# Router on unscaled rows, positions in bf16 and filler products: the routing section of a hybrid decoder on one core

## The chip, the cores and the metric

One Trainium2 chip, one of its cores. The core's engines are TensorE (PE, with its weight loads PEld), VectorE (DVE), ScalarE (ACT), GpSimd (POOL) and SyncE (SP), which here issues every DMA. The metric is the device time of one execution in microseconds (us), the median of several runs; lower is better. Everything is f32 except where bf16 is named.

## The reference, cut to what matters

Two identical layers work on 256 tokens of 1024 channels. Each layer adds three sub-layers to the residual stream `h`: token mixing, cross-attention into 256 memory tokens, and a mixture of 32 experts in 4 groups. The change sits between the second and the third.

```python
def hier_moe(xn, w_rg, b_rg, w_re, b_re, w_gu, w_dn):
    ...
    lg = jnp.dot(xf, w_rg).astype(jnp.float32) + b_rg.astype(jnp.float32)
    p_grp = jax.nn.softmax(lg, axis=-1)
    grp = jnp.argmax(lg, axis=-1)
    ...
    le = jnp.take_along_axis(le, grp[:, None, None], axis=1)[:, 0]
    top_p, top_e = lax.top_k(jax.nn.softmax(le, axis=-1), EXPERT_TOP_K)
    gate = p_grp_sel * top_p / jnp.sum(top_p, axis=-1, keepdims=True)
    ...
    gu = lax.ragged_dot(xs, w_gu, sizes)
    g_, u_ = jnp.split(gu, 2, axis=-1)
    ys = lax.ragged_dot(jax.nn.silu(g_) * u_, w_dn, sizes)
...
        h = h + cross_attention(rmsnorm(h, norm_cross[l]), rmsnorm(mem, norm_mem[l]),
                                cross_wq[l], cross_wkv[l], cross_wo[l])
        h = h + hier_moe(rmsnorm(h, norm_ffn[l]), router_group_w[l], router_group_b[l],
                         router_expert_w[l], router_expert_b[l], expert_w_gate_up[l], expert_w_down[l])
```

`rmsnorm(x, g)` is each row of x times 1/sqrt(mean of its squares), times the gain g of each channel. Every token goes to two experts of one group, and every expert's weights (6 MB) are read from HBM once a layer.

## The kernel before, in words

The kernel is one program written out by hand for each engine; the order on an engine is the order of its code, and semaphores tie the engines together. A name such as `h0_ffn` or `chosen` is such a semaphore event. The eight PSUM banks are shared by a table, `USES`: for each bank it lists its uses in order, and a use can be filled only after the one before it in the same bank has been drained.

The 256 tokens are two tiles of 128 (`tt` is 0 or 1). Behind cross-attention, PE multiplies the attention result by the output weights (`cross_out`, banks co0 to co3), and DVE adds that to `h` (`add_out`). Then, for each tile: ACT squares the rows (`squares`), DVE makes the inverse root (12 small instructions, `inverse_root`), ACT (tile 0) or DVE (tile 1) scales the rows into `xhat`, PE transposes `xhat` (`turn`, uses zT0 to zT3), DVE and ACT multiply the halves of the result by the gain into `xnT` (`turned`), and PE multiplies `xnT` by the 36 router columns (bank use `rt`).

DVE adds the bias and picks group and experts in some 20 small dependent instructions; their outcome is the table `chosen` (one where a token uses an expert). PE sums `chosen` with a triangle and with ones (use `pos`), which gives every token its place in its expert. From that DVE builds the one-hot matrix `pm` of the first pair of experts (`onehot(0)`), and PE gathers the rows of that pair by multiplying `xhat` with `pm` (`gather(0, 0)`, `gather(0, 1)`). DVE meanwhile orders the experts of each pair by size, counts the passes (`npass_ready`), and writes the tables of positions and gates of all pairs; then it multiplies the gathered rows by the gain (`gathered(0)`).

After that a loop runs over the 16 pairs of experts: gate and up products, SiLU on ACT, down products, and a product that scatters the result back to the tokens. SP loads the weights of the next pairs, each load behind the last read of the slot that it overwrites. The loads of pair 0 and most of those of pair 1 are issued before routing; the first one behind them waits for `small_read`, which PE raises when the first half of pair 0's gate and up products is done. Each layer has this sequence once. In layer 0 POOL also makes the gained memory of layer 1 (`gained(xnT, 1)`, L1212), released by `npass_ready`.

## Time and profile before

| | |
|---|---|
| median of 3 runs | 1445.12 us (1444.04 to 1446.16) |
| profiled execution, its own time | 1444.26 us |
| its span, first to last instruction | 1442.1 us |
| busy in the span: PE, DVE, ACT, POOL | 1243.6, 496.2, 243.4, 81.2 us |
| mean of PE's granted clock, as a share of full speed | 0.955 |
| mean HBM read and written | 315 GB/s |

The profiled execution's own time is 2.16 us above its span (what lies before the first and behind the last instruction), and 0.86 us below the median of the runs. Times inside the span are counted from its start. Layer 0's experts begin at about 275 us, layer 1's at about 978 us. A clock of 1.00 is 2.4 GHz and one of 0.50 is 1.2 GHz; there are only these two levels, so a share between them is a stretch with both.

### The profile page before, as it was taken

The numbers are of one execution on the slowest core, as the hardware profiler recorded it, in microseconds if no ns is written. First come the engines' busy times: TensorE is split into PE (matmuls) and PEld (weight loads), VectorE is DVE, ScalarE is ACT, GpSimd is POOL, SyncE is SP. The second block draws the span as 40 slices with busy tenths as digits, with TensorE's granted clock in tenths as the row PEclk, the third lists the DMA queues.
The fourth block names the chain that finished last, engine by engine and source line by source line (L and its number), as shares of the span: only waits on it lengthen the run. The fifth ranks groups of instructions, "written<-read, shape, count | busy, mean of one in ns | idle before, by whom it ended". The sixth has DMA issues, their size and how long they took to land.

```text
span 1442.1 us, 26136 instructions
## 1 busy us (share of the span) xinstructions
PE 1243.6 (86%) x10690; PEld 739.3 (51%) x10690; DVE 496.2 (34%) x1113; ACT 243.4 (17%) x564; POOL 81.2 (6%) x105
## 2 busy tenths in 40 slices
PE   4989898699899898878889889969988998798885
PEld 3877756444444343434468776655444443344332
DVE  4254634433223222322242654353223232222323
ACT  2003213011111111111120221221111111111111
POOL 1121300000000000000021222000000000000000
PEclk9999999699999999999999999979999999999997
DMA  8231229299999999999944113567999999999993
GB/s 337 93 147 59 102 82 428 81 426 428 427 386 428 428 427 427 428 428 429 423 174 166 60 59 117 246 279 298 425 428 385 428 429 427 429 427 427 429 428 147
DMA packets 33103, 455.11 MB, mean 316 GB/s; under 512 B 3744, under 2 KB 4000, under 8 KB 5152
## 3 DMA queue, kind: packets, MB, share of 16 engines
q1 hardware_dynamic: 33056, 454.46, 75.4%
q8 instruction: 32, 0.52, 0.1%
q14 instruction: 15, 0.12, 0.0%
HBM read 453.40 MB, written 1.05 MB: 315 GB/s over the span
## 4 chain that ended last, share of the span: by engine, by line
PE 48%; DMA 39%; DVE 6%; ACT 2%; issue 2%; SPq 1%; DVEq 0%; ACTq 0%
PE bank L459 47%; DMA share<-in_w_gu 30%; DMA share<-in_w_dn 9%; SPq L370 1%; ACT xnT L1044 1%; DVE small L1469 1%; PE bank L518 1%; DMA lb_in<-in_lb_logits 1%; DVE share L1449 1%; PE bank L677 1%; DVE rest L1760 0%; DVE h L1401 0%; ACT ring L1098 0%; DVE rest L1690 0%; ACT xhat L1025 0%
## 5 line engine op out<-in xcount | busy, mean ns | idle before, releaser
L459 PE MATMUL bank<-share,rest 128*32 128x512 f32 (+1 forms) x2560 | 309.6, 531 | 16.5 <-DMA share<-in_w_dn 16.4
L459 PE MATMUL bank<-ring,rest 128*32 128x256 f32 (+1 forms) x1792 | 184.5, 492 | 35.9 <-DMA share<-in_w_gu 30.4
L459 PE MATMUL bank<-dense,rest 128*32 128x256 f32 (+2 forms) x1824 | 190.3, 480 | 24.6 <-DMA share<-in_w_gu 21.9
L459 PE MATMUL bank<-xnT,dense 128*128 128x256 f32 (+2 forms) x960 | 162.4, 344 | 13.4 <-ACT xnT L1044 6.3
L459 PEld LDWEIGHTS bank<-share,rest 128*32 128x32 f32 x2560 | 102.7, 113 | 111.7 <-issue 94.8
L459 PEld LDWEIGHTS bank<-xnT,dense 128*128 128x128 f32 (+1 forms) x960 | 140.5, 179 | 32.2 <-issue 13.3
L459 PE MATMUL bank<-rest 96*128 96x512 f32 (+1 forms) x288 | 122.0, 579 | 34.3 <-DVE rest L1760 34.3
L459 PEld LDWEIGHTS bank<-ring,rest 128*32 128x32 f32 x1792 | 66.7, 113 | 156.0 <-issue 98.8
L1751 DVE TENSOR_TENSOR rest<-rest,bank 64x512 f32<-64x512 f32 x64 | 35.7, 558 | 322.3 <-ACT rest L1175 296.0
L459 PEld LDWEIGHTS bank<-dense,rest 128*32 128x32 f32 (+1 forms) x1824 | 69.6, 112 | 146.5 <-issue 97.8
L459 PE MATMUL bank<-rest,xhat 128*128 128x96 f32 x1088 | 142.2, 286 | 2.7 <-DVE rest L1679 2.7
L459 PEld LDWEIGHTS bank<-rest,xhat 128*128 128x128 f32 x1088 | 131.5, 198 | 18.2 <-issue 16.1
L1768 DVE TENSOR_TENSOR h<-h,bank 128x512 f32<-128x512 f32 x128 | 88.0, 688 | 57.4 <-PE bank L459 57.4
L459 PEld LDWEIGHTS bank<-rest 96*128 96x128 f32 (+1 forms) x288 | 48.8, 189 | 95.9 <-issue 95.7
L1175 ACT ACTIVATE rest<-bank 64x512 f32<-64x512 f32 x32 | 18.8, 588 | 444.7 <-PE bank L459 444.7
L1734 DVE TENSOR_TENSOR rest<-bank,par 128x384 f32<-128x384 f32 x68 | 37.8, 558 | 104.6 <-PE bank L459 103.3
L459 PE MATMUL bank<-dense,ring 128*32 128x128 f32 (+1 forms) x384 | 63.0, 380 | 0.0
L1757 DVE COPY rest<-bank 64x512 f32<-64x512 f32 x32 | 22.2, 693 | 109.0 <-PE bank L459 109.0
L459 PE MATMUL bank<-share 64*128 64x128 f32 (+2 forms) x448 | 41.3, 311 | 13.7 <-DVE ring L1544 7.2
L459 PE MATMUL bank<-dense,xnT 128*128 128x256 f32 (+2 forms) x256 | 46.4, 341 | 5.6 <-DVE share L1449 3.5
L1181 ACT ACTIVATE rest<-bank 64x512 f32<-64x512 f32 x32 | 18.9, 590 | 184.2 <-PE bank L459 184.2
L459 PEld LDWEIGHTS bank<-dense,xnT 128*128 128x128 f32 x256 | 41.1, 195 | 10.2 <-issue 3.9
(229 smaller groups left out, 954.9 us busy)
## 6 DMA issues: line engine op xcount, KB each, us to landing
share<-in_w_dn SPq DMA_DIRECT2D x64, 2048.0 KB, 19.8
ring<-in_w_gu SPq DMA_DIRECT2D x48, 2048.0 KB, 23.7
dense<-in_w_gu SPq DMA_DIRECT2D x48, 2048.0 KB, 26.6
share<-in_w_gu SPq DMA_DIRECT2D x32, 2048.0 KB, 22.9
dense<-in_w_units SPq DMA_DIRECT2D x18, 2048.0 KB, 9.0
dense<-in_w_units SPq DMA_DIRECT2D x4, 1024.0 KB, 5.1
dense<-in_w_units SPq DMA_DIRECT2D x2, 1184.0 KB, 5.8
ring<-in_w_units SPq DMA_DIRECT2D x2, 1024.0 KB, 5.8
```

Of the source, the lines that this page charges most:

```text
L370: e = sp.value_load(order_i[0:1, bass.ds(pair * 2 + s % 2, 1)], min_val=0, max_val=E - 1)
L459: return pe.matmul(out_ap, lhsT=lhsT, rhs=rhs, start=start, stop=stop, skip_group_check=True)
L518: ins = pe.transpose(bk[:, d * P:(d + 1) * P], xhat[:, tt, k * P:(k + 1) * P], ident)
L677: ins = pe.transpose(bk[:, c * P:(c + 1) * P], probs(n)[:, at:at + P], ident)
L1044: ins = act.activation(xnT[:, 4 + d, tt * P:(tt + 1) * P], bk[:, d * P:(d + 1) * P], ACT.Identity, scale=pcol(l, gain + 4 + d, 1))
L1175: act.activation(sgate[UP, 0:512], banks[2][0:HD, 0:512], ACT.Silu).then_inc(edrained[2], 1)
L1181: act.activation(ys[0:HD, 0:512], banks[4][0:HD, 0:512], ACT.Copy).then_inc(edrained[4], 1)
L1449: bank_drained(V.copy_predicated(a01[:, :, half, :], bc(lvmask[:, m, :].unsqueeze(1), 4, P), bk[:, 0:512].rearrange("p (n t) -> p n t", n= ...
L1734: V.tensor_tensor(xg[:, 4 * b:4 * b + 4, :], banks[b][:, 0:4 * ROWS].rearrange("p (d s) -> p d s", d=4), g, MUL).then_inc(edrained[b], 1)
L1751: V.tensor_tensor(hid[UP, c0:c1], sgate[UP, c0:c1], banks[b][UP, 0:c1 - c0], MUL).then_inc(edrained[b], 1)
L1757: V.tensor_copy(ys[0:HD, 512:1024], banks[4][UP, 0:512]).then_inc(edrained[4], 1)
L1768: V.tensor_tensor(hh, hh, banks[b][:, 0:512], ADD).then_inc(edrained[b], 1)
```

## The change

It has four parts, all between cross-attention and the loop over the pairs, and a small one in the preparation.

1. The router's transposes read `h` itself. The two tiles' logits are multiplied by the rows' scale afterwards, in DVE's instruction that also adds the bias. So the transposes no longer wait for the root; the scaled rows `xhat` are still made, both tiles now by ACT and behind `turned`, for the gather. `zT0` and `zT1` move to banks 4 and 5, and the first tile's transposes stand ahead of `cross_out(1)`.
2. `chosen` becomes a bf16 table, `chosen_b`, and the triangle and the ones of the positions product come from bf16 constants (`cbf`, 544 columns for 288).
3. PE multiplies constants into bank 2, whose content nobody reads: 18 products of 128x512 in bf16 ahead of the positions product, 4 behind it, and 4 behind the first gather.
4. DVE writes the tables of all pairs behind `gathered(0)`, no longer ahead of it, and POOL's product of layer 1's gained memory waits until DVE has made the gated one-hots of pair 1.

```diff
@@ USES @@
-        "wo0", "wo2", "yT0", "cq0", "yT2", "co0", "co2", "zT0", "zT2"],
+        "wo0", "wo2", "yT0", "cq0", "yT2", "co0", "co2", "zT2"],
...
-    4: ["hq", "hidT", "rk", "cmp_t"] + [f"t{n}_0" for n in range(NG)],
+    4: ["hq", "hidT", "rk", "cmp_t"] + [f"t{n}_0" for n in range(NG)] + ["zT0"],
...
@@ preparation @@
-        cbf = sb("cbf", [P, 288], BF16)
+        cbf = sb("cbf", [P, 544], BF16)
+        chosen_b = sb("chosen_b", [P, 2, 32], BF16)
...
-            sp.dma_start(rest[:, 0:1312], masks).then_inc(s_setup, 16)
+            sp.dma_start(rest[:, 0:1568], masks).then_inc(s_setup, 16)
@@ TensorE @@
-                def turn(prefix, stage, tt):
+                def turn(prefix, stage, tt, rows=xhat):
 
-                    wait(f"xhat{tt}_{stage}")
+                    wait(f"xhat{tt}_{stage}" if rows is xhat else f"h{tt}_{stage}")
...
+                turn("z", "ffn", 0, h)
                 cross_out(1)
 
                 bk = bank_free(pe, l, "rt")
-                for tt in range(2):
-                    turn("z", "ffn", tt)
+
+                def route(tt):
                     settled(f"zT{2 * tt}", f"zT{2 * tt + 1}")
                     for k in range(8):
                         ins = mm(bk[:, tt * 36:(tt + 1) * 36], xnT[:, k, tt * P:(tt + 1) * P],
                                  pcol(l, RW + k * 36, 36), k == 0, k == 7)
-                bank_done(ins, "rt")
+                    return ins
+
+                route(0)
+                turn("z", "ffn", 1, h)
+                bank_done(route(1), "rt")
+
+                def keep_clock(n):
+
+                    for i in range(n):
+                        mm(banks[2][:, 0:512], ident_b, cbf[:, 0:512], True, True)
+
+                wait_drained(pe, l, USES[2][-1])
+                keep_clock(18)
 
                 wait("chosen")
                 bk = bank_free(pe, l, "pos")
-                mm(bk[:, 0:E], tri, chosen[:, 0, :], True, True)
...
+                mm(bk[:, 0:E], tri_b, chosen_b[:, 0, :], True, True)
...
                 bank_done(ins, "pos")
+                keep_clock(4)
...
+                wait("xhat0_ffn")
+                wait("xhat1_ffn")
                 gather(0, 0)
                 gather(0, 1)
+                keep_clock(4)
                 wait("npass_ready")
@@ ScalarE @@
                 norm("ffn", 0)
+                turned("z", G_FFN, 0)
                 norm("ffn", 1)
-                turned("z", G_FFN, 0)
                 turned("z", G_FFN, 1)
+                for tt in range(2):
+                    wait(f"rstd{tt}_ffn")
+                    act.activation(xhat[:, tt, :], h[:, tt, :], ACT.Identity,
+                                   scale=rs[:, tt:tt + 1]).then_inc(ev(f"xhat{tt}_ffn"), 1)
@@ GpSimd @@
                 if l + 1 < DEPTH:
-                    wait("npass_ready")
+                    pool.wait_ge(pg_of[l], 2)
+                    alone(pool)
                     gained(xnT[:, :, :], l + 1).then_inc(ev("memG"), 1)
@@ VectorE @@
+                turned("z", G_FFN, 0)
                 norm("ffn", 0)
                 add_out("co", "ffn", 1)
-                turned("z", G_FFN, 0)
+                turned("z", G_FFN, 1)
                 norm("ffn", 1)
-                turned("z", G_FFN, 1)
...
-                bank_drained(V.tensor_tensor(rl, bk[:, 0:72].rearrange("p (t c) -> p t c", t=2),
-                                             bc(pcol(l, RBIAS, 36).unsqueeze(1), 2, 36), ADD), "rt")
+                for tt in range(2):
+                    ins = V.scalar_tensor_tensor(rl[:, tt, :], bk[:, tt * 36:(tt + 1) * 36], rs[:, tt:tt + 1],
+                                                 pcol(l, RBIAS, 36), MUL, ADD)
+                bank_drained(ins, "rt")
...
-                own("chosen", V.tensor_tensor(chosen, r_o1, r_o2, ADD))
+                V.tensor_tensor(chosen_b[:, :, :], r_o1, r_o2, ADD).then_inc(ev("chosen"), 1)
```

The first place is PE from the last values product of cross-attention to the router's products. Of before (`xhat` are the scaled rows, `par,xnT` the router's products, `dense,rest` the products of `cross_out(1)`):

```order
L459 MATMUL bank<-xnT,rest 64x128 x7
L459 MATMUL bank<-dense,rest 128x512 [waits bank0_drained,bank7_drained]
L459 MATMUL bank<-dense,rest 128x512
L459 MATMUL bank<-dense,rest 128x512 [waits bank1_drained]
L459 MATMUL bank<-dense,rest 128x512
L518 MATMUL bank<-cst,xhat 128x128 [waits bank0_drained,xhat0_ffn,bank6_drained]
L518 MATMUL bank<-cst,xhat 128x128 x3
L518 MATMUL bank<-cst,xhat 128x128 [waits bank1_drained]
L518 MATMUL bank<-cst,xhat 128x128 x3
L459 MATMUL bank<-par,xnT 128x36 [waits bank1_drained,bank0_drained]
```

Of the changed kernel, the same stretch:

```order
L462 MATMUL bank<-xnT,rest 64x128 x7
L521 MATMUL bank<-cst,h 128x128 [waits bank4_drained,h0_ffn]
L521 MATMUL bank<-cst,h 128x128 x3
L521 MATMUL bank<-cst,h 128x128 [waits bank5_drained]
L521 MATMUL bank<-cst,h 128x128 x3
L462 MATMUL bank<-dense,rest 128x512 [waits bank0_drained,bank7_drained]
L462 MATMUL bank<-dense,rest 128x512
L462 MATMUL bank<-dense,rest 128x512 [waits bank1_drained]
L462 MATMUL bank<-dense,rest 128x512
L462 MATMUL bank<-par,xnT 128x36 [waits bank4_drained,bank5_drained,bank6_drained]
```

The transposes of tile 0 have moved ahead of the four products of `cross_out(1)`, and the first router product follows those directly.

The second place is PE from the second tile's router products to the read of `npass`. Of before (`rest,cst` is the positions product, `rest,xhat` the gather):

```order
L459 MATMUL bank<-par,xnT 128x36 x7
L459 MATMUL bank<-rest,cst 128x32 [waits bank1_drained,chosen]
L459 MATMUL bank<-rest,cst 128x32 x4
L459 MATMUL bank<-rest,xhat 128x96 [waits bank5_drained,bank6_drained,bank4_drained,bank7_drained,bank3_drained,onehot_ready_0,bank2_drained,ebank0_drained_0,bank1_drained,bank0_drained]
L459 MATMUL bank<-rest,xhat 128x96 x7
L459 MATMUL bank<-rest,xhat 128x96 [waits ebank1_drained_0]
L459 MATMUL bank<-rest,xhat 128x96 x7
L914 TENSOR_LOAD npass_i [waits npass_ready]
```

Of the changed kernel (`cbf` are the bf16 constants, `bank<-cbf 128x512` the filler products):

```order
L462 MATMUL bank<-par,xnT 128x36 x7
L462 MATMUL bank<-cbf 128x512 [waits bank2_drained]
L462 MATMUL bank<-cbf 128x512 x17
L462 MATMUL bank<-chosen_b,cbf 128x32 [waits bank1_drained,chosen]
L462 MATMUL bank<-chosen_b,cbf 128x32 x4
L462 MATMUL bank<-cbf 128x512 x4
L462 MATMUL bank<-rest,xhat 128x96 [waits bank6_drained,bank7_drained,bank5_drained,xhat0_ffn,bank4_drained,xhat1_ffn,bank3_drained,onehot_ready_0,bank2_drained,ebank0_drained_0,bank1_drained,bank0_drained]
L462 MATMUL bank<-rest,xhat 128x96 x7
L462 MATMUL bank<-rest,xhat 128x96 [waits ebank1_drained_0]
L462 MATMUL bank<-rest,xhat 128x96 x7
L462 MATMUL bank<-cbf 128x512 x4
L933 TENSOR_LOAD npass_i [waits npass_ready]
```

The filler products stand in PE's queue ahead of the wait for `chosen`, ahead of the gather's wait and ahead of the read of `npass`, so each of these now also waits for them.

The third place is DVE ahead of `gathered(0)`, the two rows `rest<-bank,par` that wait for the halves of the gather. Of before (`posv` and `gates` are the tables of all pairs):

```order
L1691 TENSOR_REDUCE posv<-rest 128x16x2 [waits dve_step]
L1690 TENSOR_TENSOR rest<-rest 128x64 [waits dve_step]
L1691 TENSOR_REDUCE gates<-rest 128x16x2 [waits dve_step]
L1690 TENSOR_TENSOR rest<-rest 128x64 [waits dve_step]
L1691 TENSOR_REDUCE gates<-rest 128x16x2 [waits dve_step]
L1722 TENSOR_SCALAR posv<-posv 128x32 [waits dve_step]
L1723 COPY gates<-gates 128x32
L1684 TENSOR_TENSOR posv<-posv,cst 128x2x3 [waits dve_step]
L1729 TENSOR_LOAD npass_i
L1729 ISA x2
L1734 TENSOR_TENSOR rest<-bank,par 128x384 [waits ebank0_filled_0]
L1734 TENSOR_TENSOR rest<-bank,par 128x384 [waits ebank1_filled_0]
```

Of the changed kernel, from the count of passes on:

```order
L1743 CAST npass_i<-rest 1x1 [waits dve_step]
L1748 TENSOR_TENSOR rest<-bank,par 128x384 [waits ebank0_filled_0,npass_ready]
L1748 TENSOR_TENSOR rest<-bank,par 128x384 [waits ebank1_filled_0]
L1752 TENSOR_SCALAR rest<-rest 128x64
L1716 TENSOR_TENSOR rest<-rest 128x64 [waits dve_step]
L1717 TENSOR_REDUCE posv<-rest 128x16x2 [waits dve_step]
```

`gathered(0)` stood behind all the table rows and behind DVE's own read of `npass`; now it stands directly behind the count of passes and ahead of both.

## Rows read from the trace of the kernel before

**Rows 1.** The page, its first line.

```profile
span 1442.1 us, 26136 instructions
```

**Rows 2.** Windows: busy of PE, PEld, DVE, ACT, POOL; clock; DMA share; GB/s.

```profile
255.50:282.40 26.90, 16.11 (x99) 11.28 (x102) 16.57 (x67) 1.50 (x2) 3.60 (x1) 0.60 0.00 1
961.30:982.70 21.40, 14.26 (x99) 11.44 (x102) 13.32 (x67) 1.50 (x2) 0.00 (x0) 0.64 0.01 2
283.40:727.00 443.60, 393.46 (x3775) 190.13 (x3768) 121.51 (x236) 65.44 (x114) 0.00 (x0) 0.97 1.00 423
```

**Rows 3.** Timeline of SP's DMA issues, the first behind routing in each layer.

```profile
282.38 2.07 SPq L367 DMA_DIRECT2D ring<-in_w_gu  x2
...
982.68 2.10 SPq L367 DMA_DIRECT2D ring<-in_w_gu  x2
```

**Rows 4.** Timeline of PE, layer 0: start, us, line, op, count, idle before.

```profile
238.94 3.70 PE L459 MATMUL bank<-dense,rest 128*128 128x512 f32 x8 [0.47 <-ACT rest L1000]
243.52 1.06 PE L518 MATMUL bank<-cst,xhat 128*128 128x128 f32 x8 [0.88 <-ACT xhat L1029]
246.11 3.60 PE L459 MATMUL bank<-par,xnT 128*128 128x36 f32 x16 [1.52 <-ACT xnT L1044]
249.51 1.95 PE L518 MATMUL bank<-cst,xhat 128*128 128x128 f32 x8
252.84 3.60 PE L459 MATMUL bank<-par,xnT 128*128 128x36 f32 x16 [1.38 <-ACT xnT L1044]
...
265.03 6.13 PE L459 MATMUL bank<-rest,xhat 128*128 128x96 f32 x32 [1.35 <-DVE rest L1679]
275.70 7.98 PE L459 MATMUL bank<-ring,rest 128*32 128x512 f32 x65 [4.54 <-DVE rest L1734]
```

**Rows 5.** Timeline of PE, layer 1: first router product, gather, pair 0.

```profile
952.25 3.26 PE L459 MATMUL bank<-par,xnT 128*128 128x36 f32 x16 [1.52 <-ACT xnT L1044]
...
970.83 6.50 PE L459 MATMUL bank<-rest,xhat 128*128 128x96 f32 x32 [1.35 <-DVE rest L1679]
978.22 5.75 PE L459 MATMUL bank<-ring,rest 128*32 128x512 f32 x65 [0.90 <-DVE rest L1734]
```

**Rows 6.** Timeline of PE at full clock: bf16 constants, and a half gather.

```profile
144.97 0.40 PE L459 MATMUL bank<-cbf 128*128 128x128 bf16 x4
...
288.37 2.02 PE L459 MATMUL bank<-rest,xhat 128*128 128x96 f32 x16
```

**Rows 7.** Timeline of DVE, layer 0: logits, choice, positions, tables.

```profile
256.48 0.23 DVE L1636 TENSOR_TENSOR rest<-bank,par 128x72 f32<-128x72 f32 x1 [5.14 <-PE bank L459]
...
261.06 0.22 DVE L1658 TENSOR_TENSOR rest<-rest 128x64 f32<-128x64 f32 x1
...
263.14 0.22 DVE L1670 TENSOR_TENSOR rest<-rest 128x64 f32<-128x64 f32 x1
263.79 0.23 DVE L1694 SCALAR_TENSOR_TENSOR rest<-bank,rest 128x64 f32<-128x64 f32 x1 [0.42 <-PE bank L459]
...
267.35 0.14 DVE L1716 CAST npass_i<-rest 1x1 int32<-1x1 f32 x1
...
267.75 3.56 DVE L1690 TENSOR_TENSOR rest<-rest 128x64 f32<-128x64 f32 x1
```

**Rows 8.** Timeline of POOL, same stretch.

```profile
267.63 3.60 POOL L1212 TENSOR_TENSOR xnT<-memT,par 128x2048 f32<-128x2048 f32 x1 [98.18 <-DVE npass_i L1716]
```

**Rows 9.** Timeline of DVE in pair 1 of layer 0.

```profile
312.55 0.69 DVE L1751 TENSOR_TENSOR rest<-rest,bank 64x512 f32<-64x512 f32 x1 [6.74 <-ACT rest L1175]
```

**Rows 10.** Granted clock by windows of 1 us (column before the DMA share).

```profile
246.00:247.00 1.00, 0.89 (x5) 0.92 (x5) 0.83 (x6) 0.00 (x0) 0.00 (x0) 0.53 0.89 377
273.00:274.00 1.00, 0.00 (x0) 0.00 (x0) 0.55 (x4) 0.00 (x0) 0.00 (x0) 0.69 0.00 0
```

**Rows 11.** The chain that ended last, at the start: start, us, what.

```profile
3.44 8.99 DMA lb_in<-in_lb_logits
...
13.22 0.22 DVE cbf L1337
```

More of the change, by code:

```diff
@@ L51 @@
     3: ["xT0", "hf", "ksvs", "cmpo", "cmp_s_1"] + [f"s{n}_1" for n in range(NG)],
-    4: ["hq", "hidT", "rk", "cmp_t"] + [f"t{n}_0" for n in range(NG)],
-    5: ["ckv", "rq0"] + [f"t{n}_1" for n in range(NN)] + ["hot"] + [f"t{n}_1" for n in range(NN, NG)],
+    4: ["hq", "hidT", "rk", "cmp_t"] + [f"t{n}_0" for n in range(NG)] + ["zT0"],
+    5: ["ckv", "rq0"] + [f"t{n}_1" for n in range(NN)] + ["hot"] + [f"t{n}_1" for n in range(NN, NG)] + ["zT1"],
     6: ["q0", "rq1", "o6", "xo0", "rt"],
@@ L137, in hymba @@
         cmp_no_b = cbf[:, 256:288].rearrange("p (t c) -> p t c", t=2)
+        tri_b = cbf[:, 288:416]
+        ones_b = cbf[:, 416:544]
         def pcol(l, a, n):
@@ L220, in rtile @@
             return ys_b[:, at:at + 2 * n].rearrange("p (t c) -> p t c", t=2)
-        rl, rlog, r_in, r_o1, r_o2, chosen = [
-            rtile(a, n) for a, n in ((0, 36), (72, 36), (144, 32), (272, 32), (336, 32), (400, 32))]
+        rl, rlog, r_in, r_o1, r_o2 = [
+            rtile(a, n) for a, n in ((0, 36), (72, 36), (144, 32), (272, 32), (336, 32))]
         rexp = rtile(464, 36)
@@ L517, in turn @@
                             k = 4 * j + d
-                            ins = pe.transpose(bk[:, d * P:(d + 1) * P], xhat[:, tt, k * P:(k + 1) * P], ident)
+                            ins = pe.transpose(bk[:, d * P:(d + 1) * P], rows[:, tt, k * P:(k + 1) * P], ident)
                         bank_done(ins, f"{prefix}T{tt * 2 + j}")
@@ L1034, in norm @@
                     squares(stage, tt).then_inc(ev(f"squares{tt}_{stage}"), 1)
-                    if tt == 0:
+                    if tt == 0 and stage != "ffn":
                         wait("rstd0_" + stage)
@@ L1336, in _ @@
             V.tensor_copy(lvmask[:, :, :], mask_in).then_inc(ev("masks"), 1)
-            V.tensor_copy(cbf[:, :], rest[:, 1024:1312]).then_inc(ev("masks"), 1)
+            V.tensor_copy(cbf[:, :], rest[:, 1024:1568]).then_inc(ev("masks"), 1)
             mx, tot_, run = lbt[:, 0:2], lbt[:, 2:4], lbt[:, 4:6]
@@ L1384, in norm @@
                     own(f"rstd{tt}_{stage}", inverse_root(link, rs[:, tt:tt + 1], ssq[:, tt:tt + 1], 1.0 / D))
-                    if tt == 1:
+                    if tt == 1 and stage != "ffn":
                         V.tensor_scalar(xhat[:, 1, :], h[:, 1, :], rs[:, 1:2], None,
@@ L1693, in _ @@
                 bk = bank_full(dve, l, "pos")
+                wait("chosen")
                 link(V.scalar_tensor_tensor(r_pos, bk[:, 0:2 * E].rearrange("p (t e) -> p t e", t=2), 1.0,
-                                            chosen, ADD, MUL))
+                                            chosen_b[:, :, :], ADD, MUL))
                 bank_drained(V.tensor_copy(r_cnt, bk[:, 2 * E:3 * E]), "pos")
@@ L1716, in _, with gathered @@
                 own("npass_ready", V.tensor_copy(npass_i[0:1, 0:1], r_np[0:1, :]))
+                def gathered(n):
+                    for b in range(2):
+                        dve.wait_ge(efilled[b], n + 1)
+                        g = bc(pcol(l, G_FFN + 4 * b, 4).unsqueeze(2), 4, ROWS)
+                        V.tensor_tensor(xg[:, 4 * b:4 * b + 4, :], banks[b][:, 0:4 * ROWS].rearrange("p (d s) -> p d s", d=4),
+                                        g, MUL).then_inc(edrained[b], 1)
+                gathered(0)
                 link(V.tensor_scalar(r_pos, r_pos, -1.0, None, ADD))
@@ L1811, in constants @@
     bf = np.concatenate([
-        eye, np.where(p[None, :] > p[:, None], -1e30, 0.0), (1.0 - ok.reshape(P, 32)) * -1e30], axis=1)
+        eye, np.where(p[None, :] > p[:, None], -1e30, 0.0), (1.0 - ok.reshape(P, 32)) * -1e30,
+        (p[:, None] < p[None, :]), np.ones((P, P))], axis=1)
     s, t = p[:, None], p[None, :]
```

15 lines of the change are left out of this document (4 added, 11 removed), and 2 rows, old and new, of the table USES.

## The prediction

> **What bounds the kernel now.** I began with the busy time by windows. Through the experts of layer 0 the DMA engines are busy at a share of 1.00 and move 423 GB/s, while PE is busy 393 of 444 us [rows 2]: the loop over the pairs is paced by the stream of weights. The same view has the two stretches in which that stream stands still: 26.9 us in layer 0 and 21.4 us in layer 1 [rows 2]. Everything loaded ahead has landed by then, and the next load is issued only when PE has finished the first half of pair 0, at 282.38 and at 982.68 [rows 3]. So what routing and the first half of pair 0 get shorter comes off the end of the stream one for one, up to those gaps; what PE, DVE or ACT save inside the loop gives nothing. This is an inference from a full stream, and the sum stands on it.
>
> Next the timelines inside the gap. PE shows the staircase: output products, wait, transposes, wait, router products, transposes, wait, router products, then long waits for DVE, the gather, and pair 0 at 275.70 [rows 4]. DVE shows the other half: logits at 256.48, `chosen` at 261.28, ready for the positions at 263.36 and held up 0.42 us by PE's product of them, passes counted at 267.49, and then a table instruction of 3.56 us [rows 7], which begins 0.12 us behind POOL's product and ends with it [rows 8]. Last the clock: it falls to 1.2 GHz within 246 to 247, after PE had worked 1.06 us since 242.64, and again within 273 to 274, after the gather had ended at 271.16 [rows 4, 10]. The whole of routing runs at the lower level.
>
> **The change, part by part.** Times are those of layer 0; span times of before stand beside them.
>
> *Router.* The values products end at 238.47 (238.94 less the 0.47 of waiting). The transposes of tile 0 now follow at once, since `h0_ffn` lies behind the output products of tile 0: 1.06 us [rows 4], to 239.53. The output products of tile 1 take 3.70, to 243.23, where 242.64 was the end before: 0.6 us is given away. Router products of tile 0: at the lower clock eight take 3.60 us, and there transposes take 1.95 against 1.06 at the upper [rows 4]. Both are bound by loading 128x128 weights, and a weight costs 0.13 us at the upper level (1.06 / 8; the half gather, 2.02 / 16, agrees [rows 6]). So 16 x 0.13 = 2.1 us, to 245.3. DVE has added tile 1's output well before that. Transposes to 246.4; ACT's and DVE's halves of the gain cost what they cost now, a wait of 1.4 to 1.5 us [rows 4]; second router products 247.85 to 249.95. Before they ended at 256.44. That is 6.5 us. DVE's logits are now two instructions; the dearest like it is the 0.23 us of L1694 [rows 7], so one more is 0.2. Net 6.3 us.
>
> *Choice and positions.* DVE's row of small instructions is unchanged: `chosen` at 255.0, ready for positions at 257.1. The positions product is hidden now if PE is free, which returns the 0.42: the gather's start moves from 265.03 to about 258.3, by 6.7 us. The scaled rows of both tiles are ACT's now: two instructions behind its last gain at 247.8, with ten microseconds until the gather reads them, so nothing.
>
> *Filler products.* No row has a bf16 product of 512 columns. From below: an f32 product of 512 columns is two records of 3.70 / 8 = 0.46 us [rows 4], and a bf16 one is one record of half the bytes, so 0.23. From above: 512 columns of bf16 in four products took 0.40, their weights loaded four times [rows 6]. I take 0.23, the row with the same 512 columns. Eighteen take 4.1 us, from 249.95 to 254.1, and end 0.9 us before `chosen`. At 0.40 they last 7.2, to 257.15; then the positions (five products, 0.5 us) reach DVE at 257.7, 0.6 us late. The four behind the positions end by 257.2 at the dearest, ahead of the gather. The four behind the gather stand ahead of PE's read of `npass`: 0.9 us beside DVE's 0.88 us for the second half of the gained rows (gather's end at 977.33 to pair 0 at 978.22 [rows 5]), so nothing, or 0.7 us at 0.40. The Trainium skill, "TensorE: Matmul & The Clock Gate", section "Wait — 56ns, not 53.3ns?", gives a 512-column bf16 product 215.7 ns at the upper clock and 426.7 ns at the lower. By those figures the eighteen would take 3.9 or 7.7 us, an estimate.
>
> *Gather.* It took 6.13 us at the lower clock; two halves at the upper are 2 x 2.02 = 4.04 [rows 4, 6]. It ends at 262.4, 8.8 us earlier than 271.16.
>
> *Tables and POOL.* DVE counts the passes at 258.1 + 2.7 = 260.8 and is waiting when the gather ends, so pair 0 begins 0.88 us behind it, as in layer 1, and not 4.54 [rows 4, 5]: at 263.3, which is 12.4 us before 275.70. The tables, now behind, delay only DVE, which has nothing else until the first gate product. POOL's 3.60 us now fall into pair 1. The Trainium skill's "GPSIMD Engine Reference", section "8. Key points", says POOL shares its SBUF interfaces with VectorE, with contention for VectorE's instructions with two SBUF inputs; by that rule the wait is only moved, and if it lay on the path it would cost 3.3 us again. The rows put it elsewhere: in pair 1 DVE waits 6.74 us for ACT before its first product [rows 9], more than the 3.33 us that L1690 lost (3.56 less 0.23).
>
> *First half of pair 0.* In layer 0 it took 282.38 - 275.70 = 6.68 us, begun at the lower clock; in layer 1, at the upper, 982.68 - 978.22 = 4.46 [rows 3 to 5]. Layer 0 saves 2.2 more: 12.4 + 2.2 = 14.6 us.
>
> *Layer 1.* No POOL product, pair 0 already at the upper clock, and a first router product that took 3.26 instead of 3.60 [rows 5]. Its gather moves by 6.7 - 0.35 = 6.35, from 970.83 to 964.5, ends at 968.5, and pair 0 begins at 969.4 instead of 978.22: 8.8 us.
>
> *Preparation.* The masks are 20% longer (128 KB), on the queue ahead of the last input, whose landing starts DVE's chain [rows 11]: at 423 GB/s 0.3 us, and the cast of 544 columns for 288 some 0.3 more. Loss 0.6 us, or nothing if another wait covers it.
>
> Sum: 14.6 + 8.8 - 0.6 = 22.8 us. Both parts are below the gaps, 26.9 and 21.4. Span 1442.1 - 22.8 = 1419.3 [rows 1]; plus 2.16 outside the span 1421.5; the runs' median stood 0.86 above the profiled execution: 1422.3 us.
>
> **The rivals.**
> *The clock falls all the same (B).* Between the output products and the fillers PE has 5.3 us of work in 6.7; between the eighteen fillers and the gather it has 1.4 us of work in 4.2. The clock fell at 246 and 273 after stretches not much emptier [rows 10]. If it falls before the second router products, they take 3.6 (+1.5), the fillers run at half speed and outlast `chosen` (up to +1.7 more). If it falls before the gather, that takes 6.13 again: +2.1. One or two of these in the two layers: 1424 to 1429, about 1426. For it speaks that the second stretch resembles those two; against it, that PE is never idle for longer than 2 us in either, where it was idle for 4.5 to 5.
>
> *Fillers are dear (C).* At 0.40 us each, both delays above, (0.6 + 0.7) x 2 = 2.6 us: 1425.
>
> *The gain is hidden (D).* If another load or PE paced the loop, a restart earlier would be given back: 1443 to 1446. The share of 1.00 speaks against it [rows 2].
>
> *Slower (E).* One mechanism: the eighteen fillers hold the positions product. DVE needs it at 257.1, so they cost 18 x d - 6.65 us a layer, d being one product's time; this eats the 11.4 us a layer at d = 1.0 us, and above it the kernel is slower (at 1.2 us, by 7 us: 1452). Even an f32 record of that width is 0.46 [rows 4].
>
> **How the numbers follow.** The sum as it stands, 1419.5 to 1425: 0.52, with C's milder forms in it. B 0.33, C in full 0.04, D 0.04, E 0.02; better than 1419.5, if waits I carried over shrink too, 0.05. The range 1417 to 1429 leaves out D, E and the ends of the others. A measurement of this kernel tells 0.2% (2.9 us) from no change; only D and E are not beyond it: faster 0.94, same 0.03, slower 0.03.
>
> **What would show it.** PE's first router products directly behind the output products, and the second ending near 250; the clock column at 1.00 through the fillers and the gather; eighteen products in about 4 us ending before `chosen`; DVE's positions instruction without a wait for PE; the gather in 4.0 us; 0.9 us from it to pair 0; L1690's counterpart at 0.23 us; SP's first issue near 267.8 and, with the shift, some 23 us early in layer 1; DMA gaps of about 12.5 us in each layer. Wrong would be a clock of 0.50 in the gather, fillers still running at `chosen`, a DMA stall inside the loop that grows, or an end that moves less than the two restarts.

## The result and the profile after

| | before | changed |
|---|---|---|
| median, first comparison | 1445.64 us (4 runs) | 1422.93 us (4 runs, 1420.52 to 1425.89) |
| ratio, 95% interval | | 0.9845 (0.9824 to 0.9866) |
| ratio in two more comparisons | | 0.9849 (0.9836 to 0.9863), 0.9843 (0.9825 to 0.9861) |
| profiled execution, its span | 1442.1 us | 1421.4 us (its time 1423.15) |

1422.3 was forecast, with 1417 to 1429 around it. Lines have moved in the changed kernel: the helper of PE's products is L462, transposes L521, gathered rows L1748, the first scaled logits L1661. The busy time by windows, first line the gap of the weights' stream in layer 0, second in layer 1, third the experts of layer 0 (columns as in [rows 2]):

```profile
257.50:270.80 13.30, 11.25 (x91) 7.66 (x93) 8.55 (x44) 1.28 (x1) 0.00 (x0) 0.87 0.02 5
949.00:962.80 13.80, 12.01 (x88) 8.93 (x92) 8.06 (x40) 1.28 (x1) 0.00 (x0) 0.75 0.01 4
271.80:715.50 443.70, 393.32 (x3778) 190.68 (x3771) 125.69 (x237) 66.45 (x115) 3.60 (x1) 0.97 1.00 422
```

The gaps are 13.3 and 13.8 us, where they were 26.9 and 21.4 [rows 2], and the loop behind them is as it was: share 1.00, PE busy 393 us. So what the change gave lies ahead of the loop. SP's first issue behind routing, in each layer, 11.6 and 19.9 us earlier than in [rows 3]:

```profile
270.80 2.07 SPq L370 DMA_DIRECT2D ring<-in_w_gu  x2
...
962.83 2.10 SPq L370 DMA_DIRECT2D ring<-in_w_gu  x2
```

The timeline of PE in layer 0, from the last values product of cross-attention to pair 0; it answers [rows 4]:

```profile
239.62 1.09 PE L462 MATMUL bank<-xnT,rest 128*64 128x128 f32 x16 [0.88 <-DVE xnT L1514]
240.65 1.09 PE L521 MATMUL bank<-cst,h 128*128 128x128 f32 x8
241.58 3.60 PE L462 MATMUL bank<-dense,rest 128*128 128x512 f32 x8
245.01 1.87 PE L462 MATMUL bank<-par,xnT 128*128 128x36 f32 x16
246.72 1.07 PE L521 MATMUL bank<-cst,h 128*128 128x128 f32 x8
249.17 2.50 PE L462 MATMUL bank<-par,xnT 128*128 128x36 f32 x16 [1.39 <-ACT xnT L1063]
251.48 5.19 PE L462 MATMUL bank<-cbf 128*128 128x512 bf16 x18
256.85 0.29 PE L462 MATMUL bank<-chosen_b,cbf 128*128 128x32 bf16 x5 [0.18 <-DVE chosen_b L1684]
256.99 1.02 PE L462 MATMUL bank<-cbf 128*128 128x512 bf16 x4
260.03 5.41 PE L462 MATMUL bank<-rest,xhat 128*128 128x96 f32 x32 [2.02 <-DVE rest L1705]
265.27 1.03 PE L462 MATMUL bank<-cbf 128*128 128x512 bf16 x4
266.33 5.75 PE L462 MATMUL bank<-ring,rest 128*32 128x512 f32 x65
```

The staircase of before is gone. The router's products stand directly behind the output products, and one wait is left, the 1.39 us for ACT's half of the second tile. The gather took 5.41 us and not 4.0: the clock fell twice here, as the windows of 1 us show (the column before the DMA share), and in layer 1 the gather took 6.73:

```profile
250.00:251.00 1.00, 1.00 (x9) 1.00 (x8) 0.23 (x2) 0.76 (x2) 0.00 (x0) 0.69 0.96 410
...
260.00:261.00 1.00, 0.97 (x7) 1.00 (x8) 0.90 (x8) 0.00 (x0) 0.00 (x0) 0.81 0.00 0
```

```profile
940.46 1.95 PE L462 MATMUL bank<-par,xnT 128*128 128x36 f32 x16 [1.38 <-ACT xnT L1063]
942.24 4.05 PE L462 MATMUL bank<-cbf 128*128 128x512 bf16 x18
947.58 0.29 PE L462 MATMUL bank<-chosen_b,cbf 128*128 128x32 bf16 x5 [1.28 <-DVE chosen_b L1684]
...
950.75 6.73 PE L462 MATMUL bank<-rest,xhat 128*128 128x96 f32 x32 [2.02 <-DVE rest L1705]
```

The timeline of DVE in layer 0, which answers [rows 7]:

```profile
251.80 0.42 DVE L1661 SCALAR_TENSOR_TENSOR rest<-bank,small,par 128x36 f32<-128x36 f32 x2 [1.53 <-PE bank L462]
...
258.79 0.23 DVE L1721 SCALAR_TENSOR_TENSOR rest<-bank,chosen_b 128x64 f32<-128x64 f32 x1
...
262.35 0.14 DVE L1743 CAST npass_i<-rest 1x1 int32<-1x1 f32 x1
263.29 0.56 DVE L1748 TENSOR_TENSOR rest<-bank,par 128x384 f32<-128x384 f32 x1 [0.81 <-PE bank L462]
265.47 0.56 DVE L1748 TENSOR_TENSOR rest<-bank,par 128x384 f32<-128x384 f32 x1 [1.62 <-PE bank L462]
```

DVE reads the positions (L1721) without a wait, and it waits for the gather twice, where before the gather's end found it at its tables. POOL's product, [rows 8] before, now runs in pair 1, and so does its collision; POOL's timeline and then DVE's:

```profile
293.62 3.60 POOL L1235 TENSOR_TENSOR xnT<-memT,par 128x2048 f32<-128x2048 f32 x1 [125.11 <-DVE rest L1768]
```

```profile
293.67 3.76 DVE L1705 TENSOR_TENSOR rest<-cst,posv 128x192 f32<-128x192 f32 x1 [0.20 <-DVE rest L1768]
...
300.97 0.69 DVE L1777 TENSOR_TENSOR rest<-rest,bank 64x512 f32<-64x512 f32 x1 [3.34 <-ACT rest L1198]
```

DVE loses 3.4 us in L1705 and its wait for ACT shrinks by as much, from 6.74 [rows 9] to 3.34. The path doesn't feel it: the instruction behind that wait begins 30.17 us behind SP's first issue in both kernels (312.55 - 282.38 and 300.97 - 270.80).

One measure serves for all the traces below, the **section**: from the end of the last values product of cross-attention (here 239.62 + 1.09 = 240.71) to SP's first issue (270.80). It holds the whole change but the longer preparation, and leaves out what the clock does elsewhere. Two columns for the two layers, with the time of the gather beside each:

| profiled execution | layer 0, us | gather | layer 1, us | gather |
|---|---|---|---|---|
| before | 43.9 | 6.13 | 38.1 | 6.50 |
| changed | 30.1 | 5.41 | 30.8 | 6.73 |
| changed, second trace | 27.9 | 3.78 | 30.9 | 6.74 |
| changed, third trace | 30.8 | 6.70 | 27.9 | 3.78 |
| no fillers | 30.4 | 5.80 | 30.8 | 6.70 |
| more fillers, both traces | 27.9, 27.9 | 3.78 | 27.9, 27.9 | 3.78 |
| pair 0 made late | 33.0 | 3.78 | 36.3 | 5.41 |
| POOL's move alone | 38.1 | 6.49 | 38.1 | 6.33 |
| tables' move alone | 38.1 | 6.35 | 36.6 | 6.03 |
| router alone | 38.1 | 6.73 | 31.1 | 6.47 |
| before, with fillers | 40.3 | 3.78 | 33.8 | 3.78 |
| f32 positions, both traces | 29.6, 27.9 | 3.78 | 30.9, 30.8 | 6.75, 6.70 |

For every variant in this table, add up by how much its two sections are shorter than those of before, and take by how much its median is below that of before in the same comparison: the two agree within 1.7 us.

### The profile page after: what moved, and what is told of

Same layout as the page of the kernel before. It is cut to its first block, busy times and chain, and to the rows that moved or that the text cites. A ratio compares the mean times of both kernels' runs of the same rounds, so it can differ in the third digit from the quotient of the medians.

```text
span 1421.4 us, 26228 instructions
## 1 busy us (share of the span) xinstructions
PE 1242.3 (87%) x10732; PEld 734.5 (52%) x10732; DVE 495.2 (35%) x1113; ACT 245.9 (17%) x566; POOL 81.3 (6%) x105
## 4 chain that ended last, share of the span: by engine, by line
PE 49%; DMA 40%; DVE 6%; ACT 2%; issue 2%; SPq 1%; DVEq 0%; ACTq 0%
PE bank L462 47%; DMA share<-in_w_gu 30%; DMA share<-in_w_dn 9%; SPq L373 1%; DVE small L1493 1%; PE bank L521 1%; DMA lb_in<-in_lb_logits 1%; PE bank L680 1%; ACT xnT L1063 1%; DVE share L1473 1%; DVE rest L1786 0%; ACT ring L1117 0%; DVE h L1425 0%; ACT xnT L1117 0%; PE bank L972 0%
## 5 line engine op out<-in xcount | busy, mean ns | idle before, releaser
L462 PE MATMUL bank<-share,rest 128*32 128x512 f32 (+1 forms) x2560 | 309.9, 532 | 17.4 <-DMA share<-in_w_dn 17.4
L462 PE MATMUL bank<-dense,rest 128*32 128x256 f32 (+2 forms) x1824 | 191.6, 482 | 24.1 <-DMA share<-in_w_gu 22.3
L462 PE MATMUL bank<-ring,rest 128*32 128x256 f32 (+1 forms) x1792 | 180.9, 485 | 27.2 <-DMA share<-in_w_gu 27.1
L462 PE MATMUL bank<-xnT,dense 128*128 128x256 f32 (+2 forms) x960 | 160.8, 342 | 14.1 <-ACT xnT L1063 6.3
L462 PEld LDWEIGHTS bank<-share,rest 128*32 128x32 f32 x2560 | 102.8, 113 | 112.7 <-issue 95.8
L462 PEld LDWEIGHTS bank<-xnT,dense 128*128 128x128 f32 (+1 forms) x960 | 139.3, 178 | 32.3 <-issue 13.8
L462 PE MATMUL bank<-rest 96*128 96x512 f32 (+1 forms) x288 | 122.0, 579 | 34.3 <-DVE rest L1786 34.3
L462 PEld LDWEIGHTS bank<-dense,rest 128*32 128x32 f32 (+1 forms) x1824 | 70.0, 112 | 146.7 <-issue 98.2
L462 PE MATMUL bank<-rest,xhat 128*128 128x96 f32 x1088 | 141.7, 285 | 4.0 <-DVE rest L1705 4.0
L462 PEld LDWEIGHTS bank<-rest,xhat 128*128 128x128 f32 x1088 | 131.0, 197 | 20.3 <-issue 18.1
L462 PEld LDWEIGHTS bank<-ring,rest 128*32 128x32 f32 x1792 | 66.6, 112 | 144.5 <-issue 92.4
L462 PEld LDWEIGHTS bank<-rest 96*128 96x128 f32 (+1 forms) x288 | 48.8, 189 | 95.8 <-issue 95.7
L1748 DVE TENSOR_TENSOR rest<-bank,par 128x384 f32<-128x384 f32 x68 | 37.9, 558 | 109.3 <-PE bank L462 109.3
L462 PE MATMUL bank<-dense,ring 128*32 128x128 f32 (+1 forms) x384 | 63.2, 380 | 0.0
L462 PE MATMUL bank<-share 64*128 64x128 f32 (+2 forms) x448 | 42.6, 315 | 13.7 <-DVE ring L1568 7.2
L462 PE MATMUL bank<-dense,xnT 128*128 128x256 f32 (+2 forms) x256 | 46.4, 340 | 5.6 <-DVE share L1473 3.5
L462 PEld LDWEIGHTS bank<-dense,xnT 128*128 128x128 f32 x256 | 41.2, 195 | 10.2 <-issue 4.0
```

The costliest lines, as they stand in the source:

```text
L462: return pe.matmul(out_ap, lhsT=lhsT, rhs=rhs, start=start, stop=stop, skip_group_check=True)
L1748: V.tensor_tensor(xg[:, 4 * b:4 * b + 4, :], banks[b][:, 0:4 * ROWS].rearrange("p (d s) -> p d s", d=4), g, MUL).then_inc(edrained[b], 1)
```

## The experiments

The theory: the weights' stream restarts at the end of pair 0's first half and paces all behind it, and the change shortens the way there by fewer waits in the router, by taking DVE's tables and POOL out of it, and by a higher clock. The rivals: a hidden or moved gain, and a gain that is the fillers' or the bf16 positions'.

**The changed kernel again.** No edit.

> The changed kernel once more, as the neighbour of the three runs beside it. Its four runs so far spread over 5.4 us (1420.5 to 1425.9), those of the kernel before over 2.5. My theory is that this spread is where TensorE's clock happens to fall, a thing that differs from execution to execution: 1423, spread over 4 to 6 us, and in its trace slow stretches of the clock at other places than in the first trace. The rival, that the change itself brought the spread, expects slow stretches at the same places each time.

Measured: 1422.62 us (1418.87 to 1423.92). The spread is there again, and the same instructions ran at another clock: in the windows of the stretch from 174 to 184 us, in layer 0's mixing and far ahead of the change, the first and the second trace of the changed kernel read

```profile
174.00:184.00 10.00, 10.00 (x53) 8.31 (x54) 6.26 (x19) 2.66 (x8) 0.00 (x0) 0.66 0.64 274
```

```profile
174.00:184.00 10.00, 9.01 (x58) 6.45 (x59) 6.63 (x20) 3.71 (x12) 0.00 (x0) 1.00 0.74 316
```

So part of the spread is the clock's, outside the change. It also falls inside the section: the first trace has both gathers slow, the second only layer 1's. Of the 4.4 us between the two traces' spans, 2.2 lie ahead of layer 0's section and 2.2 in it, so the rival isn't wholly wrong: part of the spread sits in the changed code, and the variant with more fillers below has about half of it.

**No fillers.**

```diff
-                keep_clock(18)
...
-                keep_clock(4)
...
                 gather(0, 0)
                 gather(0, 1)
-                keep_clock(4)
```

> The changed kernel without its 26 filler products. My theory: the gain comes from the shorter row of waits, and the fillers save little, because the clock fell ahead of the gather in both layers with them too (gathers of 5.41 and 6.73 us). Without them TensorE is idle for some 5.5 us ahead of the positions product and again ahead of the gather, both gathers run at the lower clock (6.1 to 6.7 us), and pair 0 begins 0.9 us behind the gather: 1 to 3 us slower than the changed kernel, 1424 to 1426. Rival: the fillers carry the gain through the clock of everything behind them, 1430 or more.

Measured: 1423.99 us, ratio 0.9861 (0.9846 to 0.9876), beside 0.9849 (0.9836 to 0.9863) for the changed kernel on the same chip. The median is 1.4 us higher and the intervals overlap. The gain doesn't hang on the fillers. With the chosen number of them a gather runs at the upper clock only sometimes: in three traces of the changed kernel two gathers of six did.

What varies is not whether the clock falls but when. Six traces here have these same fillers ahead of the gather (three of the changed kernel, one of pair 0 made late, two of the f32 positions), twelve layers in all, and in each of the twelve the clock fell somewhere from the second router products to the end of the gather. Where it was low through much of the 18 fillers, they took 5.5 us and the gather 3.78, in five layers; where they ran at the upper level (3.8 to 4.1 us), the gather took 6.70 to 6.75, in five; in the last two both were slow in part (5.2 and 5.41 us). Layer 0 of the second trace is of the first kind:

```profile
249.02 5.52 PE L462 MATMUL bank<-cbf 128*128 128x512 bf16 x17
...
257.31 3.78 PE L462 MATMUL bank<-rest,xhat 128*128 128x96 f32 x32 [1.78 <-DVE rest L1705]
```

A fall within the fillers costs next to nothing (this section took 27.9 us), because behind fast ones PE only waits for `chosen`, 1.28 us in layer 1 of the first trace; a fall in the gather costs up to 3 us.

**More fillers.**

```diff
                 turn("z", "ffn", 1, h)
+                keep_clock(6)
                 bank_done(route(1), "rt")
...
-                keep_clock(18)
+                keep_clock(22)
...
                 bank_done(ins, "pos")
-                keep_clock(4)
+                keep_clock(13)
```

> The changed kernel with more fillers, so that no gap is left: 6 between the second tile's transposes and its router products (the gap is 1.39 us), 22 for 18 ahead of the positions, 13 for 4 behind them (the gap ahead of the gather is 2.0 us). If the clock falls because TensorE has too little work in these gaps, both gathers take 4.0 us and no other stretch of routing is slow: 1.4 and 2.7 us saved in the gathers, 0.6 in layer 0's router products, 4 to 5 us in all, 1418 to 1419. If the clock falls there whatever TensorE does, 1423. If the fillers are in the way, slower than 1423.

Measured: 1419.04 us, ratio 0.9826 (0.9813 to 0.984), and in the second comparison, with the expectation

> The variant with more fillers again, beside the changed kernel on one chip: 2.5 to 4 us faster than it, with both gathers in 3.8 us in the trace.

1418.93 us, ratio 0.9812 (0.9799 to 0.9826), beside the changed kernel's 1422.28 and 0.9843 (0.9825 to 0.9861). In both comparisons it is 3.4 to 3.6 us below the changed kernel, the fastest version here. PE's timeline in layer 1 of the first of them:

```profile
937.35 1.24 PE L462 MATMUL bank<-cbf 128*128 128x512 bf16 x5
938.68 1.95 PE L462 MATMUL bank<-par,xnT 128*128 128x36 f32 x16
940.46 4.92 PE L462 MATMUL bank<-cbf 128*128 128x512 bf16 x22
945.79 0.29 PE L462 MATMUL bank<-chosen_b,cbf 128*128 128x32 bf16 x5 [0.42 <-DVE chosen_b L1685]
945.93 2.96 PE L462 MATMUL bank<-cbf 128*128 128x512 bf16 x12
948.97 3.78 PE L462 MATMUL bank<-rest,xhat 128*128 128x96 f32 x32
```

The fillers take up the waits and add none: the router's products follow them at once and the gather begins where it would have. All four gathers of the two traces took 3.78 us and all four sections 27.9. With the gaps closed the clock stayed up in every one. The runs also lie closer together: over 2.3 and 3.4 us, where the changed kernel's lie over 5.1 and 6.6 in the same comparisons.

**Pair 0 made late.**

```diff
                 gather(0, 1)
-                keep_clock(4)
+                keep_clock(28)
```

> The changed kernel with 28 fillers for 4 behind the first gather, which do nothing but make pair 0 begin later: 24 more at 0.215 us are 5.2 us in each layer. The theory that the stream of expert weights restarts at the end of the first half of pair 0 and paces everything behind it expects the whole delay in the time: 10.4 us, 1433. The rival, that the stream or PE makes up for a late start (a hidden gain), expects 1423 to 1426.

Measured: 1432.86 us, ratio 0.9919 (0.9904 to 0.9934), which is 10.2 us above the changed kernel on the same chip; 10.4 had been put in. With the spread of the changed kernel's runs this is good to some 3 us, and the rival's 1423 to 1426 lies well outside that. This carries the whole sum: a microsecond ahead of the loop is about a microsecond of the time.

**POOL's move alone**, on the kernel before.

```diff
-                    wait("npass_ready")
+                    pool.wait_ge(pg_of[l], 2)
+                    alone(pool)
                     gained(xnT[:, :, :], l + 1).then_inc(ev("memG"), 1)
```

> The kernel before with one edit: POOL's product of layer 1's gained memory waits for the gated one-hots of pair 1 and not for the count of passes. DVE's table instruction falls from 3.56 to 0.23 us, so DVE is ready at 270.7 and the gather's end at 271.16 decides: pair 0 begins 3.7 us earlier, in layer 0 alone. If the shorter pause also keeps TensorE's clock up, the first half of pair 0 saves 2.2 more. My theory: 3.7 to 5.9 us faster than before, 1438.5 to 1440.5 beside 1444.3. Rival, that the product only moves its harm into pair 1: 1444.

Measured: 1440.84 us beside 1445.63, ratio 0.9968 (0.9957 to 0.9979), 4.6 us (here and below worked out from the ratio). Layer 0's section is 5.9 us shorter and layer 1's as before. Of these 3.7 are the stall and 2.2 the clock, as PE's timeline shows: pair 0 begins 0.90 us behind the gather, and its first half takes 4.45 us, at the upper clock, where it took 6.68:

```profile
265.84 6.49 PE L459 MATMUL bank<-rest,xhat 128*128 128x96 f32 x32 [1.35 <-DVE rest L1680]
273.23 5.75 PE L459 MATMUL bank<-ring,rest 128*32 128x512 f32 x65 [0.90 <-DVE rest L1735]
```

The rival, a harm that is only moved, falls.

**The tables' move alone**, on the kernel before: `gathered(0)` directly behind `npass_ready`.

```diff
                 own("npass_ready", V.tensor_copy(npass_i[0:1, 0:1], r_np[0:1, :]))
+                gathered(0)
...
                 npass = dve.value_load(npass_i[0:1, 0:1], min_val=1, max_val=MAXP)
-                gathered(0)
```

> The kernel before with one edit: the tables of all pairs behind the first gathered rows, POOL's product where it was. POOL's 3.6 us then lie beside the wait for the gather, and DVE has nothing to do for pair 0 but the gathered rows. My theory: the same stall is cured by either edit, so this saves what the POOL edit saves, 3.7 to 5.9 us in layer 0 and nothing in layer 1, where the tables ended ahead of the gather already: 1438.5 to 1440.5. Rival, that the two edits save separate things: well under 3.7 here, or gains in both layers.

Measured: 1438.94 us beside 1445.63, ratio 0.9956 (0.9943 to 0.9969), 6.4 us. Layer 0's section is 5.8 us shorter, as with POOL's move: two cures of one stall. No run has both and nothing else, but each leaves pair 0 only 0.90 us behind the gather, so the second would find nothing to cure; nor does a run take POOL's move out of the changed kernel. POOL's product still runs at its old place, beside the gather, and DVE's first gained rows fall into the middle of it and take their usual 0.56 us; one of their operands is in PSUM. POOL's and DVE's timelines:

```profile
269.31 3.60 POOL L1212 TENSOR_TENSOR xnT<-memT,par 128x2048 f32<-128x2048 f32 x1 [99.89 <-DVE npass_i L1716]
```

```profile
270.51 0.56 DVE L1721 TENSOR_TENSOR rest<-bank,par 128x384 f32<-128x384 f32 x1 [1.34 <-PE bank L459]
```

Layer 1's section is 1.5 us shorter in this trace; its first router products took 1.99 us for 3.26 and its gather 6.03 for 6.50, so that is the clock, in products that this edit doesn't touch.

**The router alone**, on the kernel before: part 1 of the change, with its lines as in the diff above, and nothing of parts 2 to 4.

> The kernel before with the first part of the change alone: the router's transposes read h, the scale goes into the logits, bank uses and order as in the changed kernel; positions in f32, no fillers, tables and POOL as before. The sum gives 6.3 us in layer 0 and 5.95 in layer 1 up to the start of DVE's choice, all of which arrives at pair 0, so 12 us faster: 1432. If the second router products run at the lower clock, 1 to 3 us of it are lost. A rival that gives the main part to the fillers and the positions expects 1438 or more.

Measured: 1434.4 us beside 1445.63, ratio 0.9929 (0.9916 to 0.9943), 10.3 us (8.2 to 12.1). The sections are 5.8 and 7.0 us shorter. In layer 0 POOL's product still stalls DVE, and the gather is slow in both layers. It is the largest single part, as the sum had it; the time shows 10.3 of the 12.8 us by which the sections are shorter, and where the rest went wasn't taken apart. Nor were the two things in this part, reading `h` and the new order of the products.

**The kernel before, with fillers**, 4 ahead of the router's first transposes, 6 behind each tile's, 22 ahead of the positions, 6 behind them, 4 behind the gather. It also loads the longer constants, as the changed kernel does.

```diff
                 for tt in range(2):
+                    if tt == 0:
+                        keep_clock(4)
                     turn("z", "ffn", tt)
+                    keep_clock(6)
...
+                keep_clock(22)
                 wait("chosen")
...
                 bank_done(ins, "pos")
+                keep_clock(6)
...
                 gather(0, 1)
+                keep_clock(4)
```

> The kernel before with fillers alone: 4 ahead of the router's first transposes, 6 behind each tile's transposes, 22 ahead of the positions, 6 behind them, 4 behind the gather. It asks what the clock is worth with the old waits. At the upper clock the router products and the second transposes save 4.2 us in layer 0 and 3.9 in layer 1, the positions 0.4; the gather saves 2.3 and 2.7, but DVE's tables then end last and hide that. So pair 0 begins 4.6 and 4.4 us earlier; if the clock also holds in layer 0 until pair 0, 2.2 more: 9 to 11 us, 1434 to 1436. The rival, that the lower clock cost little and the waits for the scaled rows were all, expects 1442 or more; one that gives everything to the clock expects 1425.

Measured: 1438.63 us beside 1445.24, ratio 0.9951 (0.9937 to 0.9964), 7.1 us and not 9 to 11. The fillers held the clock up to the gather, which took 3.78 us in both layers. Layer 1 saved 4.3 us, as expected; layer 0 only 3.6 of 4.6 to 6.8. PE's and SP's timelines of layer 0 say why:

```profile
239.20 1.09 PE L459 MATMUL bank<-xnT,rest 128*64 128x128 f32 x16 [0.88 <-DVE xnT L1502]
...
252.40 1.95 PE L459 MATMUL bank<-par,xnT 128*128 128x36 f32 x16
...
273.20 8.68 PE L459 MATMUL bank<-ring,rest 128*32 128x512 f32 x65 [6.03 <-DVE rest L1746]
```

```profile
280.57 2.07 SPq L367 DMA_DIRECT2D ring<-in_w_gu  x2
```

The faster gather only waits longer, 6.03 us, for DVE's tables, which POOL stalls; the clock falls in that wait, and the first half of pair 0 takes 7.4 us, more than the 6.68 of before. A higher clock pays nothing where another engine ends last. And the clock alone, with the old waits, is worth 7.1 us (5.2 to 9.1), a little under a third of the change's 22.7.

The same lines split the router's part. From the end of the last values product to the end of the second router products it takes 18.0 us before in layer 0, 14.1 here (240.29 to 254.35) and 10.4 in the changed kernel where the clock holds. So about half of what the new router saves can be had by the clock alone, and in the changed kernel it comes with the shorter waits.

**f32 positions** in the changed kernel.

```diff
-        chosen_b = sb("chosen_b", [P, 2, 32], BF16)
+        chosen_b = sb("chosen_b", [P, 2, 32])
...
-                mm(bk[:, 0:E], tri_b, chosen_b[:, 0, :], True, True)
+                mm(bk[:, 0:E], tri, chosen_b[:, 0, :], True, True)
...
```

> The changed kernel with the table of the chosen experts and the positions product in f32 again. The product of five matmuls takes 0.3 us in bf16 and, ten records at the upper clock, about 1.2 in f32, while DVE is busy for 2.05 us behind the choice before it reads the result. My theory: hidden, the same time as the changed kernel within 0.5 us, 1422.6. The rival, that the bf16 positions are a gain of their own, expects 1 us a layer or more: 1424.5 or above.

Measured: 1425.52 us, ratio 0.9863 (0.9848 to 0.9877), on another chip than the changed kernel's runs. By time alone this spoke for the rival. The trace spoke against it; PE's and DVE's timelines in layer 0:

```profile
257.32 1.30 PE L462 MATMUL bank<-chosen_b,cst 128*128 128x32 f32 x10
```

```profile
257.04 0.23 DVE L1684 TENSOR_TENSOR chosen_b<-rest 128x64 f32<-128x64 f32 x1
...
259.26 0.22 DVE L1721 SCALAR_TENSOR_TENSOR rest<-bank,chosen_b 128x64 f32<-128x64 f32 x1
```

The product takes 1.30 us for 0.29 and is done 0.6 us before DVE wants it. So both were run again, on one chip:

> The f32 positions again. Their first run was 2 to 3 us above the changed kernel's runs on other chips, which speaks for the rival; but in its trace DVE read the positions without a wait in both layers, and from the last values product to the restart of the stream it took 29.6 and 30.9 us, the changed kernel 30.1 and 30.8. If my theory holds, the difference was how the clock fell elsewhere, and beside the changed kernel on one chip the two agree within 1 us. If the rival holds, it is again 2 us or more slower.

> The changed kernel a third time, on the same chip as the three beside it, to settle whether the f32 positions cost anything: 1422 to 1425, and whatever this chip gives, the f32 variant should give the same.

Measured: 1422.75 us, ratio 0.985 (0.9834 to 0.9867), beside the changed kernel's 1422.28 us (1418.54 to 1425.13) and 0.9843 (0.9825 to 0.9861). They agree. The bf16 positions are worth nothing that can be measured in this kernel. The first difference had lain within the intervals of the ratios; what made it isn't shown.

## Why the prediction was right

The mechanism and the sum held, and rival B happened beside them. That the number came within 0.6 us is luck in part: the sections are 2.3 us less short than forecast, which is what B cost less what the sum was too cautious, and the steps from the profiled span to the median of the runs gave back most of the rest.

- **The stream's restart decides.** Right: 10.2 us of 10.4 put in ahead of pair 0 came out at the end (good to some 3 us), and D falls.
- **The router.** From the end of the last values product, the second router products were to end 11.5 us on; they ended 11.0 and 10.4 us on. The size was off in our favour: products that follow each other overlap, so the output products took 3.60 us and not 3.70, eight transposes 0.93 from start to start and not 1.06, eight router products 1.71 and not 2.1. DVE's second logits instruction cost 0.2, as said.
- **Choice and positions.** DVE read the positions without a wait in both layers. Two things take the wait of 0.42 us away, and either is enough: the upper clock (none in the f32 variant, nor in the kernel before with fillers) or bf16 (none in the variant without fillers, whose product ran at a clock of 0.50 and took 0.30 us). The faster router is not one of them: by itself, with f32 and the lower clock, it leaves the 0.42 in both layers.
- **Filler products.** Eighteen took 4.05 us in layer 1, 0.225 each; the estimate was 0.23. The 24 more in the variant with pair 0 made late added 5.18 us (27 records in 5.99 us, less 3 in 0.81 in the second trace of the changed kernel), 0.216 each, and with that the Trainium skill's 215.7 ns ("TensorE: Matmul & The Clock Gate", section "Wait — 56ns, not 53.3ns?") agrees. C falls. The four behind the gather end within 0.03 us of the start of pair 0 and cost nothing.
- **The gather.** The term that failed: 4.04 us was forecast, 5.41 and 6.73 were measured. This is B's second case, priced at 2.1 us a layer and measured at 1.4 and 2.7, and its first case too, 0.6 us in the router products of layer 0 for the 1.5 of its price. The price was off because the 6.13 us of before was read as a gather at the lower clock, and "the whole of routing" as running there: before, the clock was back at 1.00 from 270 on, so the last 1.2 us of that gather ran at the upper level. And the argument against B, that PE had been idle for 4.5 to 5 us where the clock fell, was a misreading: ahead of the fall at 246 its longest wait was the 1.52 us of [rows 4], and the one at 273 came some 2 us into its wait of 4.54. With a clock that holds, a gather takes 3.78 us, so this term as well had been put 0.26 too high.
- **Tables and POOL.** Right in place and size: pair 0 began 0.89 us behind the gather's end and not 4.54, and the collision went into pair 1, where it is hidden. The rule on shared SBUF interfaces in the Trainium skill ("GPSIMD Engine Reference", section "8. Key points") fits: L1705 has two inputs in SBUF and took 3.76 us for 0.36. Whether anything waits for it had to be read from the rows.
- **The first half of pair 0.** 270.80 - 266.33 = 4.47 us; 4.46 was forecast.
- **Preparation.** DVE's chain came 0.42 us later (the first product behind it at 20.70 for 20.28), not 0.6.
- **The sum.** The sections are 13.8 and 7.2 us shorter; 14.6 and 8.8 were forecast. With the clock held, as in the variant with more fillers, they are 16.0 and 10.2 shorter: the sum was 1.4 us a layer too cautious there, and B took back 2.2 and 3.0. The rest of the 20.7 us between the spans is outside the change: layer 0's mixing was 1.8 us slower on balance (3 us lost by its clock in the stretch from 174 to 184, some gained ahead of it), and 1.9 us came back behind the two restarts. What gave those 1.9 wasn't taken apart.
- **From the span to the median.** The span came out at 1421.4 us for 1419.3, 2.1 too long. The profiled execution lay 1.75 us above its span and not 2.16, and the median 0.22 below it and not 0.86 above: that is 1.5 us back, by steps that were carried over from the one profiled execution of before.

B came about in every trace of the changed kernel, and yet the median isn't in B's 1424 to 1429, because the rest of the sum was too cautious; single runs lie from 1418.5 to 1425.9.

## What to carry to other kernels

When a stream is full through a loop and stands still ahead of it, find the instruction that restarts it and count only what ends earlier there; here a microsecond was worth about one. Two cures for one stall are worth one of them, and a faster engine only waits longer if another ends last, so try the parts alone and together. If fillers are to hold TensorE's clock, fill every gap of the section up to the point where the next real product is released: filling only some of them bought 1.4 us by the medians, no more than the noise, and filling all of them 3.4 to 3.6 more.

## What the runs showed of the hardware

- The clock differs between executions of one program. The same instructions, far from the change, ran at 0.66 of full speed in one trace and at 1.00 in the next, a difference of 3 us in one place. Where the clock held in it, a section measured from one event to another inside the trace repeated to 0.1 us (27.9 four times); the medians of the f32 variant, of four runs each, differed by 2.8 us between two chips.
- A product of five bf16 matmuls with 32 columns took 0.29 us, the same in f32 1.30 us at the same clock, 1.00. At 0.50 the f32 one took 2.34 us and the bf16 one 0.30, hardly more than at the upper.
- A VectorE instruction of 192 elements a partition with two operands in SBUF, begun 0.05 us behind GpSimd's product, ended 0.2 us behind it: 3.76 us for 0.36. One of 384 elements with one operand in PSUM, begun 1.2 us into the same product, took 0.56 us, as without it.
